# A mixture layer with gathered experts on one core: head searches moved early in a round, weights to its end, samples found sooner, last V tiles in two rings, sums copied out at once

## What is computed

```python
q = einsum('td,de->te', xb, w_q).reshape(tb, PEER_HEADS, 2, D_HALF)
s = einsum('thpc,hpkc->thpk', q, sub_keys)
sv, si = lax.top_k(s, PEER_TOPK)
cand = sv[:, :, 0, :, None] + sv[:, :, 1, None, :]
cv, ci = lax.top_k(cand.reshape(tb, PEER_HEADS, 256), PEER_TOPK)
expert = (i1 * N_KEYS + i2).reshape(tb, PEER_HEADS * PEER_TOPK)
g = softmax(cv)
act = gelu(einsum('tkd,td->tk', expert_u[expert], xb))
y = einsum('tk,tkd->td', g * act, expert_v[expert])
x = x + gt2 * rms_norm(y, g_post_ffn)
```

## Time and profile before

| | us |
|---|---|
| median of 3 runs | 3461.09 |
| lowest and highest | 3460.67 to 3464.39 |
| profiled execution, its run time | 3466.26 |
| its span | 3464.5 |
| PE busy | 1794.1 (52%) |
| DVE busy | 1980.7 (57%) |
| POOL busy | 1954.1 (56%) |
| ACT busy | 358.6 (10%) |

### The profile page before, as it was taken

One profiled execution on the slowest core, in us unless ns is written; L12 is line 12 of the kernel. 1 busy time (PEld: TensorE's weight loads), 2 busy tenths in 40 slices (PEclk: granted clock), 3 DMA queues, 4 the chain that ended last, 5 costly groups with the idle time before them and its releaser, 6 DMA issues.

```text
span 3464.5 us, 25701 instructions
## 1 busy us (share of the span) xinstructions
PE 1794.1 (52%) x7978; PEld 746.8 (22%) x7978; DVE 1980.7 (57%) x5165; ACT 358.6 (10%) x908; POOL 1954.1 (56%) x2091
## 2 busy tenths in 40 slices
PE   4499998434444444444444444444444444444444
PEld 3244443311111111111111111111121111112111
DVE  0121412776666666666666666666666666677761
ACT  0202101101001101101101010001000100011000
POOL 0000000377776776677667767776777677766644
PEclk7699999666666666666666666667666676676756
DMA  9500104599999999999999999999999999999977
GB/s 354 207 0 25 73 0 164 184 395 399 409 407 381 408 409 410 375 407 407 405 375 409 404 405 379 406 407 385 403 406 410 374 410 407 408 351 378 389 294 284
DMA packets 334185, 1169.71 MB, mean 338 GB/s; under 512 B 39222, under 2 KB 46150, under 8 KB 332008
## 3 DMA queue, kind: packets, MB, share of 16 engines
q0 software_dynamic: 298256, 1090.65, 79.9%
q1 hardware_dynamic: 29368, 73.60, 5.9%
q10 hardware_dynamic: 6432, 3.90, 0.4%
HBM read 1154.54 MB, written 13.48 MB: 337 GB/s over the span
## 4 chain that ended last, share of the span: by engine, by line
DMA 21%; DVE 20%; POOL 18%; PE 11%; issue 9%; ACT 3%; POOLq 0%; ACTq 0%; DVEq 0%
DMA v_rows<-in_expert_v_dram,v_idx 15%; POOL v_rows L1083 9%; PE ps_y L1458 9%; POOL wide L1076 5%; POOL u_rows L1076 4%; DVE wide L1325 4%; DMA wide<-in_expert_u_dram,u_idx 3%; DVE u_rows L1325 3%; DMA u_rows<-in_expert_u_dram,u_idx 2%; PE ps_a L1418 1%; DVE pick L1283 1%; DVE pick L1289 1%; DVE pick_f L1294 1%; ACT L1149 1%; DVE top_i L1248 1%
## 5 line engine op out<-in xcount | busy, mean ns | idle before, releaser
L1458 PE MATMUL ps_y<-v_rows,spread 128*32 128x512 f32 x4096 | 845.4, 971 | 1171.7 <-DMA v_rows<-in_expert_v_dram,v_idx 1154.7
L1083 POOL DMA_INDIRECT v_rows<-in_expert_v_dram,v_idx x1024 | 968.1, 945 | 453.0 <-issue 296.8
L1325 DVE CUSTOM_DVE_ANT_0 wide<-wide,ps_x 128x1024 f32<-128x1024 f32 x512 | 613.1, 1218 | 390.0 <-DMA wide<-in_expert_u_dram,u_idx 380.5
L1325 DVE CUSTOM_DVE_ANT_0 u_rows<-u_rows,ps_x 128x1024 f32<-128x1024 f32 x512 | 609.5, 1218 | 276.9 <-DMA u_rows<-in_expert_u_dram,u_idx 274.9
L1076 POOL DMA_INDIRECT wide<-in_expert_u_dram,u_idx x512 | 480.7, 939 | 210.9 <-issue 135.7
L1076 POOL DMA_INDIRECT u_rows<-in_expert_u_dram,u_idx x512 | 482.2, 942 | 192.6 <-issue 126.6
L1458 PEld LDWEIGHTS ps_y<-v_rows,spread 128*32 128x32 f32 x4096 | 165.2, 150 | 1581.6 <-issue 1555.2
L1402 PE MATMUL ps_a<-wide,h2T 128*128 128x256 f32 x1152 | 299.2, 417 | 8.6 <-ACT h2T L1118 6.4
L1402 PEld LDWEIGHTS ps_a<-wide,h2T 128*128 128x128 f32 x1152 | 236.4, 211 | 133.0 <-issue 90.1
L624 POOL DMA_DIRECT2D wide<-in_w_q_dram x1 | 1.1, 1077 | 393.4 <-PE mix_pair L794 393.4
L794 PE MATMUL mix_pair<-hT,wide 128*128 128x512 f32 x512 | 220.8, 593 | 0.0
(11 more groups left out here) (219 smaller groups left out, 1630.4 us busy)
## 6 DMA issues: line engine op xcount, KB each, us to landing
ada_w<-in_w_ada_dram SPq DMA_DIRECT2D x12, 2048.0 KB, 14.7
v_rows<-in_expert_v_dram,v_idx POOLq DMA_INDIRECT x1024, 8.0
wide<-in_w_in_dram SPq DMA_DIRECT2D x1, 10240.0 KB, 38.2
x_in<-in_x_prompt_dram SPq DMA_DIRECT2D x16, 512.0 KB, 4.2
wide<-in_w_q_dram POOLq DMA_DIRECT2D x1, 8192.0 KB, 23.6
wide<-in_expert_u_dram,u_idx POOLq DMA_INDIRECT x512, 8.0
u_rows<-in_expert_u_dram,u_idx POOLq DMA_INDIRECT x512, 8.0
h_in<-h_rows SPq DMA_DIRECT2D x9, 512.0 KB, 6.8
```

The source lines that it names most:

```text
L1083: pool.indirect_dma_start(v_rows[g % RING][:, :], None, t["expert_v"][0], bass.IndirectOffsetOnAxis(ap=idx, axis=0)).then_inc(v_landed[g % ...
L1325: dve.tensor_tensor_reduce(rows[:, :], rows[:, :], x, 1.0, 0.0, ALU.mult, ALU.add, acc).then_inc(done, 1)
L1458: last = pe.matmul(ps_y[32 * j:32 * j + 32, c * HALF:(c + 1) * HALF], spread[n % 2][:, 32 * m:32 * m + 32], v_rows[(g + j) % RING][:, c * ...
```

## The change

- `heads_of`: two heads in each of rounds 0 to 19, three in 20 to 28, the last one (71) in round 29, none after. `KEPT`, the number of kept index tiles, goes from 4 to 8.
- DVE: searches after products 10 and 19, or 6, 14 and 22 with three heads. `weigh(n)` right after the last product of round n.
- TensorE: all three parts of a head in one piece after a quad, heads after quads 0, 1 and 2.
- The samples' h2 has a buffer of its own (`h2_s`), loaded at the start.
- `normalise` copies the sums from PSUM to `out_rows` first, and this copy (`y_kept`) is what the next block's opening bound waits for. Square and scaling read `out_rows`.
- ScalarE: after each Exp a Gelu of one column (`warm`); `gelu` ahead of `keep_x`.
- The last round's V tiles and the samples' go to `v_rows` and `u_rows` in turns of eight (`v_place`), sixteen buffers together. A U buffer's first use for this waits for the sample's product in it.

```diff
-    KEPT = 4
+    KEPT = 8
+    LAST = TILES * (ROUNDS - 1)
...
         def heads_of(n):
-            if n < ROUNDS - 4:
-                return range(2 * n + 4, 2 * n + 6)
-            first = 2 * (ROUNDS - 4) + 4 + 3 * (n - ROUNDS + 4)
-            return range(first, first + 3)
+            first = 2 * n + 4 + max(0, n - 20)
+            return range(min(first, HEADS * (NB + 1)), min(first + (2 if n < 20 else 3), HEADS * (NB + 1)))
+
+        def v_place(g):
+            j = g - LAST
+            if j < 0:
+                return v_rows[g % RING], v_landed[g % RING], g // RING + 1
+            if j % (2 * RING) < RING:
+                return v_rows[j % RING], v_landed[j % RING], LAST // RING + j // (2 * RING) + 1
+            return u_rows[j % RING], u_landed[j % RING], (WIDE * ROUNDS + NS) // RING + j // (2 * RING) + 1
...
             load_x1(0)
+            sp.dma_start(h2_s[:, :], scratch["h2"][NB * P:(NB + 1) * P, :]).then_inc(hs_landed, 16)
             for b in range(NB):
-                sp.wait_ge(h2_turned, 2 * b + 2)
-                sp.wait_ge(x_kept, b + 1)
-                sp.dma_start(h2_in[:, :], scratch["h2"][(b + 1) * P:(b + 2) * P, :]).then_inc(h2_landed, 16)
+                if b + 1 < NB:
+                    sp.wait_ge(h2_turned, 2 * b + 2)
+                    sp.wait_ge(x_kept, b + 1)
+                    sp.dma_start(h2_in[:, :], scratch["h2"][(b + 1) * P:(b + 2) * P, :]).then_inc(h2_landed, 16)
...
             def gather_v(g, idx):
-                if g >= RING:
+                home, landed, _ = v_place(g)
+                if g >= LAST + 2 * RING:
+                    pool.wait_ge(v_used, (g - 2 * RING) // 4 + 1)
+                elif g >= LAST + RING:
+                    pool.wait_ge(sample_dots, g - LAST - RING + 1)
+                elif g >= RING:
                     pool.wait_ge(v_used, (g - RING) // 4 + 1)
...
                 nc.scalar.activation(gate[n % (KEPT + 1)][:, :, :], gate[n % (KEPT + 1)][:, :, :], ACT.Exp).then_inc(exp_done, 1)
+                nc.scalar.activation(warm[:, :], eps[:, :], ACT.Gelu)
...
                 act.wait_ge(y_done, b + 1)
-                nc.scalar.activation(out_rows[rows, :], ps[rows, :], ACT.Square, accum_out=y_stat[rows, 0:1]
+                nc.scalar.activation(out_rows[rows, :], ps[rows, :], ACT.Copy).then_inc(y_kept, 1)
+                act.wait_ge(y_kept, b + 1)
+                nc.scalar.activation(y_junk[rows, :], out_rows[rows, :], ACT.Square, accum_out=y_stat[rows, 0:1]
                                      ).then_inc(y_ssq, 1)
...
-                dve.scalar_tensor_tensor(out=out_rows[rows, :], in0=ps[rows, :], scalar=y_stat[rows, 2:3],
-                                         in1=gate2[rows, :], op0=ALU.mult, op1=ALU.mult).then_inc(y_used, 1)
+                dve.scalar_tensor_tensor(out=out_rows[rows, :], in0=out_rows[rows, :], scalar=y_stat[rows, 2:3],
+                                         in1=gate2[rows, :], op0=ALU.mult, op1=ALU.mult).then_inc(y_scaled, 1)
...
-                places = (16, 28) if len(heads) == 2 else (12, 23, 31)
+                places = (6, 14, 22) if len(heads) == 3 else (10, 19)[:len(heads)]
                 for k in range(WIDE):
                     product(WIDE * n + k, ps_x[:, :], dot[:, n % 2, k:k + 1], dots_done)
-                    if n >= 1 and k == 1:
-                        weigh(n - 1)
...
-            weigh(ROUNDS - 1)
+                weigh(n)
...
                         if n >= 5:
-                            pe.wait_ge(y_used, n // 4)
+                            pe.wait_ge(y_kept, n // 4)
                         bound(ps_y, True)
...
-                    if first <= i < first + len(parts):
-                        f, of = parts[i - first]
-                        f(of)
-                for f, of in parts[QUADS - first:]:
-                    f(of)
+                    if i < len(heads):
+                        for f, of in head_parts(heads[i]):
+                            f(of)
```

More of the change, by code:

```diff
@@ L940, in peer @@
         eps = sb("p_eps", [P, 1])
+        warm = sb("warm", [P, 1])
         x1_in = sb("x1_in", [P, D])
         out_rows = sb("out_rows", [P, D])
+        y_junk = sb("y_junk", [P, D], BF16)
         gate2_b = sb("gate2_b", [P, D])
@@ L1079, in gather_v @@
             def gather_v(g, idx):
-                if g >= RING:
+                home, landed, _ = v_place(g)
[4 more added lines that the diff above has]
+                elif g >= RING:
                     pool.wait_ge(v_used, (g - RING) // 4 + 1)
-                pool.indirect_dma_start(v_rows[g % RING][:, :], None, t["expert_v"][0],
-                                        bass.IndirectOffsetOnAxis(ap=idx, axis=0)).then_inc(v_landed[g % RING], 16)
+                pool.indirect_dma_start(home[:, :], None, t["expert_v"][0],
+                                        bass.IndirectOffsetOnAxis(ap=idx, axis=0)).then_inc(landed, 16)
             for n in range(ROUNDS + 1):
@@ L1199, in _ @@
             for n in range(ROUNDS + 1):
+                if n >= 1:
+                    gelu(n - 1)
                 if n % 4 == 0 and 4 <= n < ROUNDS:
                     keep_x(n // 4)
-                if n >= 1:
-                    gelu(n - 1)
                 if n % 4 == 1 and n >= 5:
@@ L1335, in weigh, with emit @@
                                   flat.to_broadcast([P, 4, WIDE]), ALU.mult).then_inc(weight_done, 1)
-            def emit(ps, b, rows, gate2):
+            def emit(b, rows, gate2):
                 dve.wait_ge(y_std, b + 1)
@@ L1359, in _ @@
                 heads = list(heads_of(n))
[L1360 removed]
+                places = (6, 14, 22) if len(heads) == 3 else (10, 19)[:len(heads)]
                 for k in range(WIDE):
                     product(WIDE * n + k, ps_x[:, :], dot[:, n % 2, k:k + 1], dots_done)
[L1363 to L1364 removed]
                     if n % 4 == 1 and n >= 5 and k == 5:
[L1366 removed]
+                        emit(n // 4 - 1, slice(0, P), gate2_b)
                     if n == 0 and k in (3, 9):
@@ L1377, in _ @@
             dve.tensor_tensor(weight_s[:, :, :], act_s[:, :, :], gateT[:, :, :], ALU.mult).then_inc(sample_weight, 1)
-            emit(ps_x, NB - 1, slice(0, NS), gate2_s)
-            emit(ps_y, NB, slice(0, P), gate2_b)
+            emit(NB - 1, slice(0, NS), gate2_s)
+            emit(NB, slice(0, P), gate2_b)
         @block.tensor
@@ L1383, in turn @@
             def turn(blk):
-                pe.wait_ge(h2_landed, 16 * blk + 16)
+                rows = h2_in if blk < NB else h2_s
+                pe.wait_ge(*((h2_landed, 16 * blk + 16) if blk < NB else (hs_landed, 16)))
                 for n, ps in enumerate((ps_a, ps_b)):
@@ L1389, in turn @@
                     for k in range(4):
-                        last = pe.transpose(ps[:, k, :], h2_in[:, (4 * n + k) * P:(4 * n + k + 1) * P], ident[:, :])
+                        last = pe.transpose(ps[:, k, :], rows[:, (4 * n + k) * P:(4 * n + k + 1) * P], ident[:, :])
                     last.then_inc(h2_turned, 1)
@@ L1452, in quad @@
                 g = TILES * n + 4 * i + late
-                for j in range(4):
-                    pe.wait_ge(v_landed[(g + j) % RING], 16 * (g // RING) + 16)
+                homes = [v_place(g + j) for j in range(4)]
+                for _, landed, times in homes:
+                    pe.wait_ge(landed, 16 * times)
                 for c in range(2):
@@ L1459, in quad @@
                                          spread[n % 2][:, 32 * m:32 * m + 32],
-                                         v_rows[(g + j) % RING][:, c * HALF:(c + 1) * HALF], start=False, stop=False,
+                                         homes[j][0][:, c * HALF:(c + 1) * HALF], start=False, stop=False,
                                          skip_group_check=True)
@@ L1469, in sample_sums @@
                     g = TILES * (ROUNDS - 1) + TILES // 2 + e
-                    pe.wait_ge(v_landed[g % RING], 16 * (g // RING) + 16)
+                    home, landed, times = v_place(g)
+                    pe.wait_ge(landed, 16 * times)
                     for c in range(2):
                         last = pe.matmul(ps_x[0:32, c * HALF:(c + 1) * HALF], spread_s[:, 32 * e:32 * e + 32],
-                                         v_rows[g % RING][:, c * HALF:(c + 1) * HALF], start=False, stop=False,
+                                         home[:, c * HALF:(c + 1) * HALF], start=False, stop=False,
                                          skip_group_check=True)
@@ L1498, in _ @@
                 heads = list(heads_of(n)) if n < ROUNDS else []
-                first = 1 if len(heads) == 2 else 0
-                parts = [x for hd in heads for x in head_parts(hd)]
                 for i in range(QUADS):
```

7 lines of the change are left out of this document (5 added, 2 removed).

## The result

The changed kernel takes 3449.11 us (median of 6 runs, 3445.23 to 3450.24) against 3462.74 for the kernel before on the same chip. The ratio is 0.9957 [0.9944, 0.9969]: 0.4% faster, where 2.6% was forecast. The span is 3447.9 us, 16.6 less than before.

A forecast was written before the change was run, and what follows sets the result against it. Bound by DMA transfer at about 409 GB/s, POOL's issue only 3% faster. Terms -43 - 23 - 40 + 12 + 2 + 1.1 = -91 us took the span from 3464.5 to 3373.5; forecast median 3370, range 3356 to 3398.

The forecast's parts named there:

- Head parts in one piece after a quad: TensorE's three steps per head, 6.2 us, fit between quads; nearly free, 2 us put on it, at most 36.
- listed for SP who waits behind whom: SP's queue of h2, x_kept and sample-row loads: claimed that no one waits, no cost.
- Rival F: TensorE waits in order through three ScalarE round trips per head; at 12 us a head 249 us lost, 3619; chance 0.02.
- Sums copied out: Block starts: the new bound waits for ScalarE's copy alone, so six bandwidth dips go; -43 us and part of 23.
- Searches and weights: Rounds 29 to 31: earlier searches and weights at the round's end remove the late starts; -23 us.
- the wait for the indices: Before the last V tiles: POOL's wait for sample indices goes, POOL going on without the 30.6 us.
- Budgets: Allowed lateness in the rounds: a quad may start 3.9 us late, a product 14.0 us after its tile lands.
- Start: Round 0: one more search before product 24 delays the first V gather to 714.0; +12 us, between 0 and 15.3.
- Last V tiles and end: Last stage: no index wait and sixteen buffers, -40 us; uncovered copy before the last square at the end, +1.1.
- rival G: An old wait returns in its place each block and only the tail is won: 3436; chance 0.02.
- the prediction's 0.67 us: POOL issues beside DVE's scaling with two SBUF inputs: each costs at most this, inside the 2.7 us queue, so nothing.

The follow-up runs named there:

- e1_order: The changed kernel with an odd head's index copy and Exp (`picked`) moved after the next head's copies in ScalarE's order: 3399.41 us, ratio 0.9815.
- e12_waitscale: e3_both with a block's opening bound waiting for DVE's scaling again in place of ScalarE's copy: 3416.18 us, ratio 0.9868.
- e3_both: The changed kernel with ScalarE's `picked` after the next head's copies and round 0's searches back after products 16 and 28: 3384.86 us, ratio 0.9773.
- e7_lateweigh: e3_both with the weights of a round back behind the second product of the next round: 3384.81 us, ratio 0.9769.
- e6_nowarm: e3_both without the one-column Gelu after each Exp: 3380.87 us, ratio 0.9758.
- e5_close: e3_both with three-head rounds searching after products 6, 10 and 14 in place of 6, 14 and 22: 3425.91 us, ratio 0.9884.
- the first pair: The changed kernel with only round 0's searches put back after products 16 and 28, against the changed kernel: 3437.34 us against 3449.11.

## Why the prediction was wrong

**The step that failed is "Head parts in one piece after a quad".** It gave the step 2 us, at most 36; it cost 50 (e1_order). It counted the three steps with their copies as 6.2 us, and 6.2 is right: in the kernel after head 45 takes 2336.55 to 2342.79, the end of the copy at 2342.41. What it left out is what else stands in ScalarE's queue between two heads. It listed for SP who waits behind whom and found nobody, and didn't make the same list for ScalarE, whose program has `picked` behind each odd head. That was harmless while the odd head was a round's last; `heads_of` made it the middle one in five rounds. The kernel before had the same order in its rounds 28 to 31, with three heads, and TensorE waited no longer than 0.7 us for a copy there: parts stood a quad apart, and the third head's came after quad 6, when the second's search was over or nearly so. So it took both, this order and all heads placed ahead of the searches; e1_order cures it by the order, and a run that spreads the parts again wasn't made. The copy's wait is set by DVE's place for the search (product 14), not by anything on TensorE. Rival F had the right chain (TensorE waits in order through ScalarE) with the wrong price: it asked how long a head takes if all heads are slow, in place of which head's copy can be held, and by what.

**Sums copied out: right in mechanism, too large.** 43 us were taken for six starts, 7.2 each. Rounds 5 to 19 with four starts gave 19.4, or 4.8 each, and e12_waitscale prices seven at 31.3, or 4.5. The working of round 25 came true to a tenth in round 9, and a start's round itself goes from 89.1 to 82.5 us (iteration 9 to 10). But the round before it goes from 85.8 to 87.0. This isn't a loss that the dip had hidden: in e12_waitscale, where the dips are back, iterations 8, 12 and 16 take 86.5, 88.0 and 87.4 us, as in the kernel after (87.0, 87.6, 87.5), against 85.8, 86.0 and 86.5 before. It comes from another part of the change, which no run separates. The wait alone is worth 4.5 a block, and the dip was 7.4 deep: a dip's whole depth isn't the price of its last cause.

**Searches and weights: right in sum.** Rounds 28 to 31 take 48.7 us less in e3_both; 30.6 of these are the wait for the indices, so 18 of the 23 came. What the weights' place was said to add did not appear: it is worth nothing (e7_lateweigh), nor is the warm-up (e6_nowarm).

**Budgets: right.** The 14.0 us for DVE's lag told that places 6, 14, 22 hold, and e5_close shows what lies beyond. (Behind a search after product 22 nine products are left, not ten; 9 x 1.42 = 12.8 us still cover the 10.4.)

**Start: right in kind, low.** 12 us were taken, with 15.3 as the bound. Iterations 0 to 5 took 14.9 more, and 14.6 came back with the old places (e3_both against e1_order), 11.8 in the first pair. The first V gather was issued at 718.97 in place of 714.0. Search 4 began at 682.61, 3.2 us later than the 679.38 it was reckoned from: the first gather of all had started 1.5 us later in this execution, and the warm-up had given searches 3 and 5 an Exp table load of 1.28 us each that they hadn't had. The step's chain is there: DVE waits 8.16 us at 682.61 for head 4's scores.

```profile
673.22 1.22 DVE L1350 CUSTOM_DVE_ANT_0 wide<-wide,ps_x 128x1024 f32<-128x1024 f32 x1
...
682.61 0.49 DVE L1268 MAX8 top_v<-s_sb 128x8 f32<-128x128 f32 x2 [8.16 <-ACT s_sb L1160]
```

**Last V tiles and end: right.** Of 40 - 1.1 us, 30.6 (the indices) + 15.4 (iteration 32) - 4.8 (the end) = 41 came. At the end the last tile lands 10.1 us after its issue, in the kernel before 5.9: the DMAs are busy all the time now (409 GB/s from 3339 to 3420, before 266). POOL goes on into iteration 32 without a break, which answers to the earlier trace rows:

```profile
3363.50 0.93 POOL L1105 DMA_INDIRECT v_rows<-in_expert_v_dram,v_idx  x1 [0.31 <-issue]
3364.74 0.94 POOL L1093 DMA_INDIRECT wide<-in_expert_u_dram,s_idx  x1 [0.30 <-issue]
```

With the failed step put at 50 in place of 2, and the block starts at 31 for all seven, the prediction's own sum is 3461 - 31 - 18 - 40 + 15 + 50 + 1 = 3438; measured 3449. Of the remaining 11 us 1.7 are the base, 3462.7 in this comparison. Some 6 more are block starts and searches: 19.6 + 4.8 + 18.1 = 42.5 us came in e3_both from iteration 5 to 32 without the wait for the indices, and not 31 + 18, for round 29's start stands in both terms. The rest is open; the stages are of single profiled executions, and that of the kernel before ran 3.5 us above its median. A loss still to be had is the round with the sample rows: iteration 29 takes 88.7 us in e3_both, where SP's eight loads and the stored rows now fall into a full stream and not into the wait for the indices.

The measured 3449 lies nearer to rival G's 3436 than to the forecast, but G isn't what happened: the gains came, and a new loss took most of them away.

## What to carry to other kernels

When a step in one engine's order waits on another engine, write down all that the other engine has in its own order at that point, and what each of those waits for, for every variant of the round; a copy of 0.4 us cost 11.8 because of what stood in front of it. When the number of items in a loop body changes, look again at pieces placed by parity or "after the last". And price a dip by the round's whole length with and without its cause, not by its depth.

## What the runs showed of the hardware

The load of an activation table isn't held by the wait of the operation that needs it: in the kernel before it starts at 2743.36, 4.2 us ahead of its gelu. Loading it early by hand therefore won nothing where the engine waits anyway (e6_nowarm).

```profile
2743.36 1.28 ACT L1170 ACT_TABLE_LOAD   x1
2747.57 0.23 ACT L1170 ACTIVATE act_u<-dot 128x32 f32<-128x32 f32 x1 [2.92 <-DVE dot L1325]
```

Issues beside operations of DVE with two SBUF operands grew by more than the prediction's 0.67 us: 1.91 us in the kernel after, beside the block's scaling (1405.43 to 1406.72) and addition, against 0.94; the longest, at 2077.7, takes 1.99.

```profile
1405.62 1.91 POOL L1093 DMA_INDIRECT wide<-in_expert_u_dram,u_idx  x1 [0.30 <-DVE dot L1350]
```

The Trainium skill, page "SBUF — State Buffer", section "SBUF: two separate sides", says that such an operation takes a port pair against GpSimd for the whole instruction, and the trace agrees in kind; the sum of all issues grew by 6 us over the kernel, with at most one such long issue a block (four of 1.5 to 2.0 us before the last stage), and no run here shows a loss from it.

The eight sample loads cost more than their bytes. Each spreads one row over 32 partitions, 128 KB; SP issues them from 3069.54 in e3_both, and a store and a load of 512 KB at 3073.15 and 3073.61. With the DMAs busy all the time, 318 GB/s were moved from 3070 to 3080, not 409. Whether their size or the repeated row does it wasn't separated.

```profile
3070.00:3080.00 10.00, 4.73 (x22) 1.41 (x22) 3.51 (x6) 2.05 (x3) 7.37 (x8) 0.80 1.04 318
```
